# A three-block model on one core: input stage, layer norms, one mixer norm and some small fetches rearranged

## The reference

```python
# first block
mod = silu(c) @ w_ada + b_ada;  shift, scale, gate = split(mod, 3)
h = rms_norm(x, norm_in_gain) * (1 + scale) + shift
q, k, v, z_attn, xbc, dt_raw, z_ssm = split(h @ w_in, splits)
y_attn = rms_norm(stick_breaking_attention(q, k, v), sb_norm_gain) * silu(z_attn)
y_ssm  = rms_norm(ssd_scan(silu(conv(xbc)), dt, ...) * silu(z_ssm), ssm_norm_gain)
x = x + gate * (concatenate([y_attn, y_ssm]) @ w_out)
x = rms_norm(x, norm_f_gain)                      # the norm "norm_f"
# second block, layer 0: rwkv7; layer 1: sparse attention
xx = token_shift(x) - x;  xm = x + xx * mix       # six mixes
r, k, v = einsum(xm[:3], w_rkv)
... decay, a, g from small "lora" products; scan over time; group norm; @ w_o
x = layer_norm(ALPHA * x + h, ln_g, ln_b)         # ln00, then ln10
f = conv_ffn(x, ...)                              # up, conv, silu, down
x = layer_norm(ALPHA * x + f, ln_g, ln_b)         # ln01, then ln11
```

## Time and profile before

| | |
|---|---|
| time, median of 3 runs | 2344.52 us (2340.64 to 2351.3) |
| time of the profiled execution | 2341.65 us |
| its span, first to last instruction | 2339.9 us |
| PE busy | 2147.3 us (92%) |
| DVE busy | 1306.6 us (56%) |
| ACT busy | 774.5 us (33%) |
| POOL busy | 271.0 us (12%) |
| one step of the rkv chain in its steady part (24 matmuls) | 5.44 us |
| mean granted clock of PE | 0.958 |
| read from memory | 154.69 MB, 67 GB/s over the span |

### The profile page before, as it was taken

How to read it: one execution, slowest core, us unless ns; L and a number is a source line. 1 busy time by engine, 2 the same in 40 slices (tenths; PEclk the granted TensorE clock), 3 DMA queues, 4 the chain that set the end, 5 groups by cost and what they waited for, 6 DMA issues and landing times. The chain is left out here.

```text
span 2339.9 us, 36921 instructions
## 1 busy us (share of the span) xinstructions
PE 2147.3 (92%) x16050; PEld 1652.7 (71%) x16050; DVE 1306.6 (56%) x1837; ACT 774.5 (33%) x1119; POOL 271.0 (12%) x181
## 2 busy tenths in 40 slices
PE   7998989999979956999888999999967988999998
PEld 3885767887858716999555888887534666888885
DVE  2334756665445586555456776634396536667534
ACT  2434654444223450000124222322244624222322
POOL 0000003334400042111320000000005300000000
PEclk9998999999989987999989999999888999999999
DMA  6322002212222200000111333232210021333331
GB/s 269 99 99 82 1 10 81 70 58 66 97 61 98 84 18 3 4 4 4 37 39 60 92 98 99 91 99 88 95 63 1 1 72 53 95 95 99 92 98 46
DMA packets 47042, 159.22 MB, mean 68 GB/s; under 512 B 5328, under 2 KB 7376, under 8 KB 46880
## 3 DMA queue, kind: packets, MB, share of 16 engines
q1 hardware_dynamic: 44832, 150.84, 20.1%
q10 hardware_dynamic: 2048, 6.01, 0.8%
HBM read 154.69 MB, written 2.14 MB: 67 GB/s over the span
## 5 line engine op out<-in xcount | busy, mean ns | idle before, releaser
L924 PE MATMUL banks<-up_x_high,up_w_high 128*128 128x512 f32 x1056 | 412.1, 390 | 8.5 <-DVE up_w_low L918 3.9
L926 PE MATMUL banks<-up_x_high,up_w_low 128*128 128x512 f32 x1056 | 411.5, 390 | 0.0
L925 PE MATMUL banks<-up_x_low,up_w_high 128*128 128x512 f32 x1056 | 411.4, 390 | 0.0
L918 DVE TENSOR_TENSOR up_w_low<-weight_ring,up_w_high 128x1024 fp32r<-128x1024 f32 x132 | 161.7, 1226 | 270.6 <-ACT up_w_high L913 270.6
L913 ACT CAST up_w_high<-weight_ring 128x1024 fp32r<-128x1024 f32 x132 | 138.3, 1049 | 362.7 <-PE banks L926 338.2
L924 PEld LDWEIGHTS banks<-up_x_high,up_w_high 128*128 128x128 f32 x1056 | 198.4, 188 | 53.3 <-issue 11.6
L926 PEld LDWEIGHTS banks<-up_x_high,up_w_low 128*128 128x128 f32 x1056 | 198.4, 188 | 41.3
L925 PEld LDWEIGHTS banks<-up_x_low,up_w_high 128*128 128x128 f32 x1056 | 198.4, 188 | 40.5
L1444 POOL TENSOR_TENSOR hproj_w_low<-weight_ring,hproj_w_high 128x1024 fp32r<-128x1024 f32 x43 | 106.0, 2466 | 513.6 <-ACT hproj_w_high L1252 513.6
L977 DVE SCALAR_TENSOR_TENSOR act<-banks,cols,act 128x511 f32<-128x511 f32 (+1 forms) x176 | 131.9, 749 | 6.2
L1132 PE MATMUL banks<-hproj_x_high,hproj_w_high 128*128 128x512 f32 x224 | 90.2, 403 | 5.2 <-DVE hproj_x_low L1397 3.4
(11 more groups left out here) (452 smaller groups left out, 4379.5 us busy)
## 6 DMA issues: line engine op xcount, KB each, us to landing
weight_ring<-in_up SPq DMA_DIRECT2D x88, 512.0 KB, 3.6
weight_ring<-in_down SPq DMA_DIRECT2D x44, 512.0 KB, 3.6
weight_ring<-in_w_ada SPq DMA_DIRECT2D x24, 512.0 KB, 6.1
weight_ring<-in_w_rkv SPq DMA_DIRECT2D x24, 512.0 KB, 3.3
weight_ring<-in_w_in SPq DMA_DIRECT2D x20, 512.0 KB, 3.4
weight_ring<-in_w_out SPq DMA_DIRECT2D x16, 512.0 KB, 3.3
weight_ring<-in_w_q SPq DMA_DIRECT2D x8, 512.0 KB, 6.1
weight_ring<-in_w_k SPq DMA_DIRECT2D x8, 512.0 KB, 3.2
```

The source lines that it names most:

```text
L918: nc.vector.tensor_tensor(w_low[:, n % 2, :], ring[:, i % RING, :], w_high[:, n % 2, :].bitcast(f32), ALU.subtract).then_inc(wl_made, 1)
L924: nc.tensor.matmul(PS[:, bank, :], high, x_high[:, k, :], start=start, stop=False)
L925: nc.tensor.matmul(PS[:, bank, :], high, x_low[:, k, :], start=False, stop=False)
L926: return nc.tensor.matmul(PS[:, bank, :], low, x_high[:, k, :], start=False, stop=stop)
```

## The change

1. First stage. The square sums go between the chunks of `ada_rows` (one ahead of each of the chunks 4 to 11); the two halves of a chunk go to different column groups of PE. DVE refines the root before it takes the scale. ACT casts the chain's first two weight chunks, and DVE makes their remainders, before the shift is complete. The rest of the constants (`squares`, and 128 instead of 1280 columns of `late`) is fetched after these casts, and waited for behind the chain.
2. Layer norms. Two more matmuls on constants stand in PE's list, ahead of and behind the mean's ones-matmul. In the feed-forward stages DVE makes the first two `w_low` after the subtractions and not before the norm.
3. norm_f. Squares, square sums, root and Newton move into the block of w_out, behind its last products; the rkv stage only scales. Its six `KEEP_AWAKE` matmuls go.
4. `fetch_lora` is issued by ACT at the first step of job k of the chain and not at its start. The transfers of the group norm are issued by SP.
5. `r *= sig` is done by DVE, behind `kx *= tmp`, and not by POOL.

```diff
-        def split_chain(name, *jobs, before=None):
+        def split_chain(name, *jobs, before=None, early=False):
...
-                    if s >= 2 or not before:
+                    if s >= 2 or not (before or early):
                         high_of_weights(act, s)
...
+                    nc.tensor.matmul(PS[:, 7 - turn, :], mat("ones"), squares[:, 0:T], start=True, stop=True)
                     pe.wait_ge(parts_taken, 1)
                     nc.tensor.matmul(means, mat("ones"), partial, start=True, stop=True).then_inc(summed, 1)
+                    nc.tensor.matmul(PS[:, 7 - turn, :], mat("ones"), squares[:, 0:T], start=True, stop=True)
...
-            def vector_stats(dve):
+            def vector_stats(dve, meanwhile=lambda dve: None):
...
+                meanwhile(dve)
                 dve.wait_ge(rooted, 1)
...
-                w, g = next_chunk(pe), k % 4 * 32
+                between(k)
+                w = next_chunk(pe)
                 for half in range(2):
+                    g = (k % 2 * 2 + half) * 32
...
+            def early_sums(k):
+                if k == 4:
+                    pe.wait_ge(mats_in, 16)
+                if k >= 4:
+                    square_sum(k - 4)
+
+            def late_sums(k):
+                if k < 4:
+                    square_sum(k + 4)
+                if k == 4:
+                    pe.wait_ge(rows_taken, 2)
+                    ada_cols(lambda n: aux[:, n * P:(n + 1) * P], 4, 0).then_inc(cols_made, 1)
...
+            ada_rows(pe, 0, between=early_sums)
+            ada_rows(pe, 2, between=late_sums)
...
+            qkv["high_of_weights"](act, 0)
+            qkv["high_of_weights"](act, 1)
+            act.dma_start(squares[:, n_early:], A["squares"][:, n_early:]).then_inc(rest_in, 16)
+            act.dma_start(late[:, 0:P], A["late"][:, 0:P]).then_inc(rest_in, 16)
             act.wait_ge(mod_taken, 3)
-            act.wait_ge(rest_in, 32)
...
+            qkv["low_of_weights"](dve, 0)
             dve.wait_ge(cols_made, 2)
             nc.vector.tensor_tensor(mod[:, 0:8], PS[:, 6, 0:8], b_ada[:, 0:8], ALU.add).then_inc(mod_taken, 1)
+            qkv["low_of_weights"](dve, 1)
...
-                norm["vector_stats"](dve)
+                norm["vector_stats"](dve, first_weights)
...
+                pe.wait_ge(x_made, 5)
+                for i in range(8):
+                    pe.wait_ge(f_squared, i + 1)
+                    mm = nc.tensor.matmul(sum_bank, mat("ones"), sq_o(i), start=i == 0, stop=i == 7)
+                mm.then_inc(f_summed, 1)
...
+                for i in range(8):
+                    act.wait_ge(x_made, i + 1)
+                    nc.scalar.activation(sq_o(i), x[:, i, :], ACT.Square, scale=D ** -0.5).then_inc(f_squared, 1)
+                act.wait_ge(f_summed, 1)
+                nc.scalar.activation(root, sum_bank, ACT.Abs_reciprocal_sqrt, bias=eps_col).then_inc(f_rooted, 1)
...
+                newton(dve, f_rooted, f_fixed)
...
+        norm_f = {**norm_f, "tensor": nothing, "scalar_stats": nothing, "vector_stats": nothing}
...
-        def fetch_lora(act):
+        def fetch_lora(act, k):
+            if k:
+                return
...
+                                          ready=fetch_lora if b == 1 else None, prepare=mixed(xm, xx, b) if b else normed_and_mixed)
...
+                nc.vector.tensor_tensor(ALL(r), ALL(r), ALL(sig), ALU.mult).then_inc(prepared, 1)
...
-                pool.wait_ge(decayed, 1)
-                pool.wait_ge(rk_made, 8)
-                nc.gpsimd.tensor_tensor(ALL(r), ALL(r), ALL(sig), ALU.mult).then_inc(prepared, 1)
```

More of the change, by code:

```diff
@@ L637, in first_tensor, with square_sum @@
         def first_tensor(pe):
+            def square_sum(i):
+                pe.wait_ge(squared, i + 1)
+                mm = nc.tensor.matmul(PS[:, 5, :], mat("ones"), sq[:, i, :], start=i == 0, stop=i == KT - 1)
+                if i == KT - 1:
+                    mm.then_inc(summed, 1)
+            def early_sums(k):
[9 more added lines that the diff above has]
+                    ada_cols(lambda n: aux[:, n * P:(n + 1) * P], 4, 0).then_inc(cols_made, 1)
             pe.wait_ge(c_ready, 1)
             pe.wait_ge(zeroed, 4)
-            ada_rows(pe, 0)
-            pe.wait_ge(mats_in, 16)
-            for i in range(KT):
-                pe.wait_ge(squared, i + 1)
-                mm = nc.tensor.matmul(PS[:, 5, :], mat("ones"), sq[:, i, :], start=i == 0, stop=i == KT - 1)
-            mm.then_inc(summed, 1)
-            pe.wait_ge(rows_taken, 2)
-            ada_cols(lambda n: aux[:, n * P:(n + 1) * P], 4, 0).then_inc(cols_made, 1)
-            ada_rows(pe, 2)
+            ada_rows(pe, 0, between=early_sums)
+            ada_rows(pe, 2, between=late_sums)
             pe.wait_ge(rows_taken, 4)
@@ L681, in first_vector @@
             b_ada = cols[:, COL_AT["b_ada"]:COL_AT["b_ada"] + 24]
+            dve.wait_ge(rooted, 1)
+            nc.vector.scalar_tensor_tensor(out=fix, in0=PS[:, 5, :], scalar=eps_col, in1=root, op0=ALU.add, op1=ALU.mult).then_inc(fixed, 1)
+            dve.wait_ge(fixed, 1)
+            nc.vector.scalar_tensor_tensor(out=fix, in0=fix, scalar=-0.5, in1=root, op0=ALU.mult, op1=ALU.mult).then_inc(fixed, 1)
+            dve.wait_ge(fixed, 2)
+            nc.vector.scalar_tensor_tensor(out=root, in0=fix, scalar=1.5, in1=root, op0=ALU.add, op1=ALU.mult).then_inc(fixed, 1)
+            dve.wait_ge(fixed, 3)
             dve.wait_ge(cols_in, 16)
@@ L713, in program @@
         v_tok = v[:, :, :].rearrange("p a b -> p (a b)").rearrange("p (b c) -> p b c", b=NB)
-        run_stage(norm_in, split_chain("qkv",
-                  dict(k_tiles=8, rhs=rows(h), ready=shift, by="act", take=lambda e, n, b: nc.scalar.mul(q[:, n, :], b, HD ** -0.5)),
-                  dict(k_tiles=8, rhs=rows(h), by="act", take=copy_act(rows(k_))),
-                  dict(k_tiles=8, rhs=rows(h), by="act", tokens=True, take=copy_act(lambda n: v_tok[:, n // 2, n % 2 * T:(n % 2 + 1) * T]))))
+        qkv = split_chain("qkv",
+                          dict(k_tiles=8, rhs=rows(h), ready=shift, by="act", take=lambda e, n, b: nc.scalar.mul(q[:, n, :], b, HD ** -0.5)),
+                          dict(k_tiles=8, rhs=rows(h), by="act", take=copy_act(rows(k_))),
+                          dict(k_tiles=8, rhs=rows(h), by="act", tokens=True, take=copy_act(lambda n: v_tok[:, n // 2, n % 2 * T:(n % 2 + 1) * T])),
+                          early=True)
+        constants = {"tensor": lambda pe: None, "vector": lambda dve: None, "scalar": lambda act: act.wait_ge(rest_in, 32)}
+        run_stage(norm_in, qkv, constants)
         restore("k")
@@ L962, in vector, with first_weights @@
             def vector(dve):
-                for n in range(2):
-                    low_of_weights(dve, n)
-                norm["vector_stats"](dve)
+                def first_weights(dve):
+                    for n in range(2):
+                        low_of_weights(dve, n)
+                norm["vector_stats"](dve, first_weights)
                 norm["vector_tile"](dve, 0)
@@ L1569, in program @@
         a_ = F[6]
-        run_stage({"tensor": nothing, "vector": nothing, "scalar": fetch_lora}, chain,
+        run_stage(chain,
                   {"tensor": hidden_tensor, "vector": hidden_vector, "scalar": hidden_scalar})
@@ L2063, in _ @@
             def _(sp):
+                for dst, src, landed in ((of_heads, A["of_heads"], heads_in), *((t, A["to_heads"], heads_in) for t in to_heads),
+                                         (g2_[0], A["w_g2"][0:80, :], g2_in), (g2_[1], A["w_g2"][80:160, :], g2_in)):
+                    sp.dma_start(dst, src).then_inc(landed, 16)
                 stream(sp)
```

26 lines of the change are left out of this document (8 added, 18 removed).

## The result

The changed kernel takes 2314.61 us (median of 4 runs, 2312.72 to 2320.8) against 2344.45 us for the kernel before in the same comparison (4 runs, 2340.64 to 2351.3): a ratio of 0.9874, 95% interval 0.9845 to 0.9903, so 29.8 us faster. The profiled execution took 2314.69 us, with a span of 2312.9 us. That is 27.0 us under the span of before; the forecast counted 26.1 between the same two.

A forecast was written before the change was run, and what follows sets the result against it. PE, busy 92% of the span, was taken as the bound: its products plus its idle places. Terms 8.8 + 8.2 - 1.1 - 1.9 + 4.2 + 2.6 + 5.3 = 26.1 us off 2341.65 gave 2316 us, range 2305 to 2328.

The forecast's parts named there:

- the case that was called likeliest: Whole kernel: time as summed, with its small errors, 2309 to 2320 us; chance 0.58.
- First stage, 8.8 us: Program start: PE starts the qkv chain at about 41.4 instead of 50.20 us; gain 8.8, bounds 7.5 and 11.6.
- norm_f, 8.2 us: w_out to rkv chain: sums directly behind w_out, first rkv product at 674.2 instead of 682.43 us; gain 8.2.
- Clock behind 13 idle us, a loss of 1.1: Start of rkv chain: PE idles 13 us before it and the clock drops; loss 1.1 us, bounds 0 and 3.
- the rule named beside it: Start of rkv chain: the Trainium skill's rule that an idle PE is throttled again and the next work starts cold.
- The rival with a clock that stays at half level: rkv chain after 13 us without work: 5.4 us more per step, 2446 us with all 24; slower, chance 0.02.
- Transfers in job k, a loss of 1.9: rkv chain, step 9: ACT's seven transfers delay casts and copies, so PE waits; loss 1.9 us, bounds 0 and 4.
- `r *= sig`, 4.2 us: Scan preparation: DVE's 128 x 64 instruction falls from 8.87 us, one 4.33 us multiplication is added; gain 4.2, bounds 3 and 4.5.
- Layer norms, 7.9 us (2.6 and 5.3): Layer norms: earlier copy gains 1.3 us in each of two feed-forward stages; four norms' square sums fall 33.8 to 28.5.
- Group norm's transfers, nothing: Group norm: transfers leave ACT where it waits for DVE anyway and SP has a full ring; no gain or loss.

The follow-up runs named there:

- the experiment with the early constants: Changed kernel with the rest of the constants (1.57 MB) fetched right behind the input again, as before; 2317.14 us.
- the kernel without fillers: Changed kernel without the two extra matmuls on constants in each layer norm, weight remainders left behind the subtractions; 2318.15 us.
- the last experiment: Changed kernel with the first two weight remainders of each feed-forward stage again ahead of the layer norm on DVE; 2313.66 us.

## Why the prediction was right

The median of 2314.6 is 1.4 us from the 2316 forecast, and the case that was called likeliest is the one that came. Part of this closeness is luck. The sum was taken off the profiled execution, 2.8 us under the median; taken off the median it would give 2318.4. And what the sum had wrong or left out, up to 3 us each way, cancels to 0.9, as the count at the end shows. By its terms:

- **First stage, 8.8 us: 8.5 measured** (7.6 to 9.1 over the profiles with either start). DVE became the one waited for, as said, and the start came at 41.7 and not 41.4. The sums ended at 29.3 as forecast, by two errors that cancel: a chunk with its sum takes 2.01 us and not 1.83 (the first two 2.56, with a wait of 0.48 for the chunk), but I counted the eight from chunk 4 at 14.67, and the first sum stands ahead of it, at 13.03. The chunks did not wait for slots; held up by the constants they did, and it cost 2.5 us (the experiment with the early constants), so the later fetch is part of the gain.
- **norm_f, 8.2 us: 8.2 measured.** The forecast had 24.9 us from the additions to the product (674.2 - 649.3), and so it is. The experiments split it: 4.5 for the place of the norm and 3.7 for the transfers. The 10.07 us of the old sums was one draw of the clock, though; where they took 8.85 the gain would have been 7.0.
- **Clock behind 13 idle us, a loss of 1.1: nothing measured in this pair.** This step failed. I took the 2.8 us of the qkv chain's start for what longer idling costs; the figure came from these two windows, and the rule named beside it does not give it. But the rkv chain loses 1.6 us behind 13.3 idle us and lost 1.7 behind 3.2, and the qkv chain loses 1.6 us now (6 us at 0.73) behind 4.5 idle us and lost 2.8 behind 3.4. The other profiles show that the length of the idle time does not set it. The same start of the qkv chain, behind 3.4 us, lost 1.4, 1.5, 2.6 and 2.9 us of its first 8 in the four kernels that have it unchanged (2.6 in the kernel before). The rkv chain lost 1.7 us behind 3.2 in all five profiles, 1.8 behind 8.9, 1.4 and 1.6 behind 17.0, and behind 13.3 us 1.6 and 1.8, but 3.0 in the kernel without fillers and in the one with the weights first, neither of which changes anything ahead of this chain:

```profile
665.30:673.30 8.00, 8.00 (x23) 6.30 (x24) 4.74 (x9) 0.00 (x0) 0.00 (x0) 0.62 0.00 0
```

This is the view by windows of the latter kernel; the changed kernel shows 0.80. So the loss varies between 1.4 and 3.0 us in these profiles, and the 1.1 forecast lay inside that spread. The rival with a clock that stays at half level is out: in every profile the second 8 us of the chain show 1.00.

- **Transfers in job k, a loss of 1.9: 0.3 us of waiting measured, about 1.0 by the whole chain.** Mis-sized. I let the issues begin when the weight cast ends; the first two run beside it (706.31, with the cast at 706.29), and ACT is held 2.87 us and not 3.73. And ACT's eight copies took 4.00 us, not 4.50.
- **`r *= sig`, 4.2 us: 4.3 measured**, in the changed kernel and alone. DVE's 128 x 64 instruction took 8.87 us beside POOL's multiplication and takes 0.27 without it. It ended with POOL's, at 883.3 and 883.2 us. The Trainium skill (SBUF — State Buffer, SBUF: two separate sides) says that DVE and GpSimd share a pair of ports under an exclusive lock, held for a whole instruction; the two rows agree.
- **Layer norms, 7.9 us (2.6 and 5.3): 6.6 measured**, from the first mean matmul to the last square sum. Each mechanism is there to the tenth, 1.3 us twice (the last experiment) and 33.8 to 28.5 for the sums. But by norm it is 2.8, 0, 3.9 and 0 us. In the second norm the sums won 1.5 us, and the matmuls ahead of them, which now ran at low clock, lost as much: the two records of the first filler took 2.00 us where the others' took 1.12. That is a draw as well: this norm took 14.1 us here and in two other kernels with fillers, 12.5 in the remaining five, and with 12.5 the term would have measured 8.1. The fourth had its sums at 7.13 us before already.
- **Group norm's transfers, nothing:** from the group norm to the output product 58.8 us before and after.

Two profiles, one of either kernel, give this account. What the sum did not have: the scan took 2.1 us more, the first block 0.7 more, and the last two stages won 9.5 us, 2.9 more than their norms. They hold the same products as before; what differs is the granted clock. Against the terms: 0.3 less at the start, 2.4 more in chain and preparation (3.6, where 4.2 - 1.1 - 1.9 = 1.2 was forecast), 1.3 less in the norms, 2.9 more beside them, 2.8 less in scan and first block; that is 26.1 + 0.9 = 27.0. That scan and first block are drawn anew in each execution is argued from the other kernels: the scan, whose instructions are the same in all, took 238.8 to 242.2 us, and the first block, behind its first product nearly the same, 597.5 to 606.4. The Trainium skill (TensorE: Matmul & The Clock Gate, What's actually happening) has the gate judge in windows that run free of the program; by that rule a spread from run to run is expected. The spread is there, but no run here shows that it comes from this. The 2.9 us beside the norms are of this kind too: the other kernels with fillers have between 3.2 us won there and 0.7 lost.

## What to carry to other kernels

Between two stages, list what the waiting engine's release really needs and do that first; what is merely due soon (a second remainder, the last tiles) goes behind it. The change left 7.5 us there, which showed in its profile as DVE work ahead of the instruction that ended PE's wait. A term of 1 to 3 us is proved by the distance between two landmarks of the trace (18.58 and 19.87 us, twice), when the whole time is not able to show it.

## What the runs showed of the hardware

ACT issues a transfer every 0.5 to 0.6 us, and does so beside its own cast: the first two of seven (706.31 to 707.48) ran while a cast did (706.29 to 707.34). The other five held its next cast back by 2.87 us. In the middle of the chain this cost PE 0.32 us of waiting; at the start of the stage, with nothing under way, the seven cost it 3.7 us. Six fillers at full clock ahead of the chain did not keep the clock up when 3.2 us of idling followed, in five profiles; behind 1.41 us it stayed up, in one. Behind the same 13.3 idle us the same chain lost 1.6 or 3.0 us of its first 8 to the clock. And fetching 1.57 MB of constants at a time when weights stream at some 410 GB/s did not cost what it would by volume (1.57 MB at this rate, 3.8 us): the start came 2.5 us later, with PE waiting 1.38 and 0.78 us for two chunks.
